# A two-layer hybrid decoder step: the order of work around the ConvFFN's openings, pairs, stage change and round changes

## The chip, the cores and the metric

The kernel runs on one core of a Trainium2 chip. The metric is the device time of one execution in microseconds (us), median of several runs. TensorE (PE) multiplies, VectorE (DVE), ScalarE (ACT) and GpSimd (POOL) do elementwise work, and SyncE (SP) issues nearly all DMA transfers.

## The reference, cut to what matters

Two layers run for a prompt of 1024 tokens and 64 sample tokens together. Each layer is a mixer (attention and a recurrence in layer 0, a chunk MLP in layer 1) followed by a gated ConvFFN, which is what the change touches:

```python
def conv_ffn(xn, buf, w_g, w_u, w_c, b_c, w_d):
    g = xn @ w_g                                  # 1024 -> 3072
    gc, new_buf = causal_dwconv(g, buf, w_c, b_c) # 3 taps along the tokens
    return (jax.nn.gelu(gc) * (xn @ w_u)) @ w_d, new_buf
...
yp = yp + conv_ffn(rmsnorm(yp, g_ffn[l]), ...)
```

All is float32. The outputs are the two activations and the caches and states.

## The kernel before, in words

Activations lie with features on partitions: eight tiles of 128 features by 1088 tokens. A float32 product is made of three products of rounded operands: every operand is split into a high part (a ScalarE copy to fp32r, "hi") and a low part (the rest, a subtraction, "lo"), and hi·hi, lo·hi and hi·lo are added in PSUM.

The ConvFFN uses a seven-product scheme (Winograd's form of Strassen's) over 2 × 2 blocks. A **job** is one such scheme: seven **groups** of matmuls i = 0..6, in `multiply` (line 2190), with the activation operands B21, B11, T1, T2, B22, NT4, T3 and seven weight blocks. Four weight blocks come from the sums S1 to S4 of the raw weight quarters (`block_sum`, L2115). `block_hi` (L2288, ScalarE) and `block_lo` (L2121) split them; VectorE takes the lows 2, 3, 4, 6 and GpSimd 0, 1, 5. Jobs 0 to 23 are the up and gate stage: 12 pairs, an even job for the gate and an odd one for up, 24 matmuls a group. Jobs 24 to 39 are the down stage: four rounds of four jobs, 18 matmuls a group. Sums go to PSUM banks 6 and 7, except those of job 0, which GpSimd makes into two SBUF buffers (`first_sums`, L2084 to L2093).

**Opening.** While the projection ahead (`Output`, matmuls of L148) ends, VectorE evacuates its tiles (L1827), and makes the sums T1, T3, T2, NT4 of the activation halves (L2440, L2428, L2434, L2458); L2449 makes their lows. The reciprocal root of the mean square comes from squares (L1652 on ScalarE, added by GpSimd at L1661) and three matmuls with ones (L1669) into banks 6 and 7.

**Pair.** Results of a group leave PSUM by a ScalarE copy (L2307) and a VectorE addition (`add_out`, L2480). The gate is scaled (L2486), goes through the convolution (first tap on ScalarE, L2325; the other two in `conv_taps`, L2492 and L2494; samples, L2505 to L2509), gelu (L2336), a scaling on GpSimd (L2127), and is multiplied with the up half in `hidden_tile` (L2514). GpSimd makes the four sums of the hidden halves (`hidden_sum`, L2524), and SP stores tiles and sums in DRAM.

**Down stage.** For each round seven pieces (3 × 544 columns) are loaded back (L2026), split by `piece_hi` (L2345, ScalarE) and `piece_lo` (L2132; VectorE makes five, GpSimd T2 and NT4), and VectorE adds each group's result to the residual tile (`add_residual`, L2543), whose tiles are reloaded from `x_spill` (L1994). Job 27, 31, 35 end a round; the next round's pieces are split during them.

The order on each engine is written out by hand, and each engine runs its list strictly in order; semaphores tie the lists together. SP's list is `sync`. A group of PE waits for its weight lows, for its operand lows, and for the VectorE addition that frees the PSUM bank which it writes:

```python
if i in (1, 4, 6):
    dve.wait_ge(self.dve_out, base + {1: 1, 4: 4, 6: 6}[i])   # add_residual
...
elif i == 3:
    pe.wait_ge(self.dve_out, dve + 1)                         # up/gate stage: after add_out(n, 1)
elif i in (0, 1):
    pe.wait_ge(self.dve_out, dve - 1 + i)                     # down stage
```

## Time and profile before

| what | value |
|---|---|
| median of 3 runs | 2687.48 us (2686.31 to 2687.71) |
| profiled execution, its own time | 2689.28 us |
| its span | 2687.6 us, mean granted TensorE clock 0.974 |
| busy: PE, DVE, ACT, POOL | 2494.0, 1790.8, 1149.8, 1038.4 us |
| FFN of layer 0: opening, pairs, down stage | from about 628, from about 700, 1189 to 1494 us |
| FFN of layer 1: the same | from about 1805, from about 1877, 2365 to 2679 us |

Times in rows count from the start of the span. A value in brackets is how long the engine had been idle before the instruction and what ended that idle time. The granted clock is 1.00 at 2.4 GHz and 0.50 at 1.2 GHz.

### The profile page before, as it was taken

The numbers are of one execution on the slowest core, as the hardware profiler recorded it, in microseconds if no ns is written. First come the engines' busy times: TensorE is split into PE (matmuls) and PEld (weight loads), VectorE is DVE, ScalarE is ACT, GpSimd is POOL, SyncE is SP. The second block draws the span as 40 slices with busy tenths as digits, with TensorE's granted clock in tenths as the row PEclk, the third lists the DMA queues.
The fourth block names the chain that finished last, engine by engine and source line by source line (L and its number), as shares of the span: only waits on it lengthen the run. The fifth ranks groups of instructions, "written<-read, shape, count | busy, mean of one in ns | idle before, by whom it ended". The sixth has DMA issues, their size and how long they took to land.

```text
span 2687.6 us, 46186 instructions
## 1 busy us (share of the span) xinstructions
PE 2494.0 (93%) x18693; PEld 2387.7 (89%) x18693; DVE 1790.8 (67%) x2118; ACT 1149.8 (43%) x1851; POOL 1038.4 (39%) x663
## 2 busy tenths in 40 slices
PE   8999998897899999988988999996999999988888
PEld 7878876697899999988988999996999999988888
DVE  6456566547687777786667434548677768777774
ACT  5575666434444444443223433434443444433331
POOL 3244332225344545452223412244535455442221
PEclk9999999998999999999999999998999999998999
DMA  5101118642223222255332211121223232274322
GB/s 177 56 24 43 42 32 283 232 151 81 73 79 109 90 94 101 82 189 185 121 112 78 57 35 52 55 90 56 94 89 106 77 106 93 99 258 136 127 81 79
DMA packets 214176, 276.98 MB, mean 103 GB/s; under 512 B 11437, under 2 KB 158998, under 8 KB 210894
## 3 DMA queue, kind: packets, MB, share of 16 engines
q1 hardware_dynamic: 212910, 271.83, 30.4%
q8 instruction: 149, 2.44, 0.4%
q10 hardware_dynamic: 576, 2.10, 0.2%
q14 instruction: 61, 0.50, 0.1%
q0 software_dynamic: 480, 0.11, 0.0%
HBM read 203.57 MB, written 70.43 MB: 102 GB/s over the span
## 4 chain that ended last, share of the span: by engine, by line
PE 60%; DVE 10%; issue 5%; DMA 2%; ACT 1%; POOL 1%; SPq 0%; ACTq 0%; DVEq 0%; POOLq 0%
PE psum_all L2190 46%; PE psum_all L2798 6%; PE psum_all L148 6%; DVE x_residual L2492 2%; DVE psum_all L2115 1%; DVE x_residual L2486 1%; DVE x_residual L2480 1%; DMA pair_raw_ffn<-in_w_down_dram 1%; POOL down_x_ffn L2132 1%; DVE down_x_ffn L2132 1%; DVE ffn_x_sums L2440 0%; DVE x_residual L2543 0%; PE psum_all L2850 0%; PE psum_all L2814 0%; DVE block_s L2121 0%
## 5 line engine op out<-in xcount | busy, mean ns | idle before, releaser
L2190 PE MATMUL psum_all<-ffn_x,blocks 128*128 128x272 f32 x5760 | 748.6, 291 | 65.3 <-DVE x_residual L2480 34.6
L2190 PEld LDWEIGHTS psum_all<-ffn_x,blocks 128*128 128x128 f32 x5760 | 738.2, 191 | 70.9 <-issue 55.3
L2190 PE MATMUL psum_all<-down_x_ffn,blocks_down 128*128 128x272 f32 x2880 | 395.6, 299 | 74.4 <-issue 44.4
L2190 PEld LDWEIGHTS psum_all<-down_x_ffn,blocks_down 128*128 128x128 f32 x2880 | 386.4, 199 | 80.3 <-issue 79.9
L2307 ACT COPY x_residual<-psum_all 128x544 f32<-128x544 f32 x192 | 117.8, 614 | 403.5 <-PE psum_all L2190 399.1
L2543 DVE TENSOR_TENSOR x_residual<-x_residual,psum_all 128x544 f32<-128x544 f32 (+1 forms) x224 | 178.6, 798 | 152.9 <-PE psum_all L2190 151.5
L113 POOL TENSOR_TENSOR w_lo_part<-w_raw,w_hi_part 128x1024 fp32r<-128x1024 f32 x52 | 126.9, 2440 | 356.0 <-ACT w_hi_part L97 356.0
L2480 DVE TENSOR_TENSOR x_residual<-x_residual,psum_all 128x544 f32<-128x544 f32 x144 | 130.4, 906 | 123.6 <-PE psum_all L2190 119.8
L2127 POOL TENSOR_TENSOR x_residual<-x_residual,rms_scale 128x1088 f32<-128x1088 f32 x48 | 134.8, 2809 | 180.6 <-ACT x_residual L2336 180.6
L2121 DVE TENSOR_TENSOR blocks<-psum_all,blocks 128x512 fp32r<-128x512 f32 x138 | 94.9, 688 | 118.4 <-ACT blocks L2288 118.4
L2798 PE MATMUL psum_all<-operand_a,w_hi_part 128*128 128x364 f32 (+1 forms) x672 | 169.9, 330 | 0.0
L909 PE MATMUL psum_all<-in_hi_even,w_hi_part 128*128 128x384 f32 (+1 forms) x456 | 157.0, 344 | 1.2 <-DVE xb_padded L1430 0.6
L1363 POOL TENSOR_TENSOR take_then_weights<-take_then_weights,x_residual 128x511 f32<-128x511 f32 (+3 forms) x96 | 95.0, 1001 | 159.3 <-DVE x_residual L1395 119.1
L2190 PE MATMUL psum_all<-ffn_x,block_a 128*128 128x272 f32 x1152 | 152.4, 288 | 0.0
L2190 PE MATMUL psum_all<-ffn_x,block_s 128*128 128x272 f32 x1152 | 151.9, 287 | 0.0
L909 PE MATMUL psum_all<-in_lo_even,w_hi_part 128*128 128x384 f32 (+1 forms) x456 | 149.3, 327 | 0.0
L909 PE MATMUL psum_all<-in_hi_even,w_lo_part 128*128 128x384 f32 (+1 forms) x456 | 149.0, 327 | 0.0
L2524 POOL TENSOR_TENSOR x_residual<-x_residual 128x544 f32<-128x544 f32 x96 | 144.3, 1503 | 9.8 <-DVE x_residual L2514 2.6
L2190 PEld LDWEIGHTS psum_all<-ffn_x,block_a 128*128 128x128 f32 x1152 | 147.2, 188 | 0.5
L2190 PEld LDWEIGHTS psum_all<-ffn_x,block_s 128*128 128x128 f32 x1152 | 147.0, 188 | 0.0
L1395 DVE TENSOR_TENSOR_SCAN x_residual<-x_residual,all_ones 128x512 f32<-128x512 f32 (+3 forms) x96 | 91.8, 990 | 73.2 <-ACT x_residual L1183 73.2
L2798 PEld LDWEIGHTS psum_all<-operand_a,w_hi_part 128*128 128x128 f32 x672 | 119.3, 188 | 0.5
(372 smaller groups left out, 4835.5 us busy)
## 6 DMA issues: line engine op xcount, KB each, us to landing
staging_ffn<-hidden_spill SPq DMA_DIRECT2D x54, 816.0 KB, 6.1
hidden_spill<-x_residual SPq DMA_DIRECT2D x24, 1088.0 KB, 4.0
w_raw<-in_w_gate_dram SPq DMA_DIRECT2D x24, 1024.0 KB, 5.6
x_residual<-in_w_up_dram SPq DMA_DIRECT2D x24, 1024.0 KB, 5.2
pages<-in_cache_k_dram SPq DMA_DIRECT2D x64, 256.0 KB, 3.6
pages<-in_cache_v_dram SPq DMA_DIRECT2D x64, 256.0 KB, 5.6
x_spill<-x_residual SPq DMA_DIRECT2D x24, 546.0 KB, 5.5
x_residual<-x_spill SPq DMA_DIRECT2D x24, 546.0 KB, 5.8
```

The lines of the kernel that those rows point to most:

```text
L113: pool.tensor_tensor(dst if dst is not None else self.lo[:, par, :], self.raw[:, par, :], (hi if hi is not None else self.hi[:, par, :]).b ...
L148: mm = pe.matmul(bank[:, c, 0:width(c)], w, x[:, chunk(c)], start=(k == 0 and step == 0), stop=(k == last and step == 2))
L909: mm = pe.matmul(bank(key, 0, b - a), wt[:, n % 2, col], xt[:, k, a:b], start=k == 0 and s == 0, stop=k == KT - 1 and s == 2)
L1363: pool.tensor_tensor(t[:, 0:n - 1], t[:, 0:n - 1], k[:, 1:n], ALU.mult).then_inc(weighted, 1)
L2121: eng.tensor_tensor(self.block(n, i, 1).rearrange("p (q c) -> p q c", c=P), self.source(n, i), self.block(n, i, 0).bitcast(F32).rearrange( ...
L2127: pool.tensor_tensor(self.conv[:, r, :], self.conv[:, r, :], self.core.rb[:, 0:USED], ALU.mult).then_inc(self.gr_ready, 1)
L2190: mm = pe.matmul(self.core.ps[:, b + h, 0:HB], wt[:, q * P:(q + 1) * P], xt[:, q, HB * h:HB * (h + 1)], start=first and at == 0, stop=at = ...
L2307: act.copy(self.half(self.target(n, r), h).rearrange("p (h n) -> p h n", h=2), self.group(name)).then_inc(self.act_out, 1)
L2480: dve.tensor_tensor(dst, dst, src, ALU.add).then_inc(self.dve_out, 1)
L2524: pool.tensor_tensor(dst, x, y, op).then_inc(self.hsum, 1)
L2543: dve.tensor_tensor(dst, dst, src, ALU.add).then_inc(self.dve_out, 1)
L2798: mm = pe.matmul(self.core.ps[:, self.lane_bank(f), 0:width(c)], wm[:, is_u, col], xm[:, k, chunk(c)], start=k == 0 and s == 0, stop=k == ...
```

## The change

It reorders the hand-written lists and moves some instructions to another engine; all results are the same.

- Job 0's sums are made by VectorE into banks 6 and 7 (`first_weights_dve`, ahead of the evacuation of tile 6), with its lows 2, 3, 4, 6 on VectorE too. GpSimd keeps lows 0, 1, 5. The sums of squares go to the banks of group "d". The square scratch moves by 1024 bytes, so that it no longer overlaps block 3.
- Job 1's sums and most of its lows move into the opening's list. The load of job 1 waits for the first NT4 sum, which is now that of tile 1, instead of all four.
- `conv_taps` becomes `conv_tap`, one tap each: the addition of the up job's group 1 stands between the two taps of the first half, and sums and lows between those of the second.
- The last pair's hidden tiles and hidden sums go to the end of VectorE's list for job 24 (`down_first`).
- All piece lows are VectorE's. At a round change B21, B11, T1, T2 are made during the last job of the round, B22, NT4, T3 during the first of the next, whose sums for the job after come later.
- SP loads pieces 7 to 10 (the next round's first four) before the last pair's stores.

```diff
@@ Output.vector
         for m in range(KT):
-            if m == KT - 1:
+            if m == KT - 2:
+                self.ffn.first_weights_dve(dve)
+            elif m == KT - 1:
                 self.ffn.open_dve(dve)
@@ Ffn.sync
-        sp.wait_ge(self.sum_lead, self.T_MADE[NT4][3])
+        sp.wait_ge(self.sum_lead, self.T_MADE[NT4][0])
         self.load(sp, 1)
...
         self.load_next(sp, n + 2)
+        for g in range(7, 11):
+            self.load_piece(sp, g)
         self.store_hidden(sp, PAIRS - 1)
...
-            if r < ROUNDS - 1:
+            if 0 < r < ROUNDS - 1:
                 for i in range(4):
                     self.load_piece(sp, 7 * (r + 1) + i)
@@ Ffn.gpsimd
+        self.block_lo(pool, 0, 0)
+        self.block_lo(pool, 0, 1)
         self.add_squares(pool, KT - 2)
-        pool.wait_ge(*self.out.job_done(KT - 2))
-        self.first_sums(pool, "S1")
-        for i in (1, 0, 2):
-            self.block_lo(pool, 0, i)
         pool.wait_ge(self.act_lead, self.T_HI[T1])
...
-        self.first_sums(pool, "S4")
         self.add_squares(pool, KT - 1)
-        pool.wait_ge(self.s_sum, KT - 1)
-        for i in (3, 4, 5):
-            self.block_lo(pool, 0, i)
+        self.block_lo(pool, 0, 5)
...
-        self.block_lo(pool, 0, 6)
...
-                if n == JOBS1 - 1 and i in (5, 6):
-                    self.piece_lo(pool, 0, (T2, NT4)[i - 5])
-                elif turn and i in (T2, NT4):
-                    self.piece_lo(pool, r + 1, i)
@@ Ffn.opening (PE)
         self.multiply(pe, 0, 3)
+        pe.wait_ge(self.act_out, 1)
         self.sums_pe(pe, (0, 1))
...
         pe.wait_ge(self.t2_lo, 2)
+        pe.wait_ge(self.s_root, 3)
         self.multiply(pe, 0, 5)
@@ Ffn.opening_act
+        for i in range(4):
+            self.block_hi(act, 0, i)
         self.tile_act(act, KT - 2)
-        self.block_hi(act, 0, 1)
-        self.block_hi(act, 0, 0)
...
-        self.block_hi(act, 0, 2)
-        self.tile_act(act, KT - 1)
-        self.block_hi(act, 0, 3)
         act.wait_ge(self.sum_lead, self.T_MADE[T2][2])
         act.activation(self.operand(0, T2, 0)[:, 0:3], self.temp(T2)[:, 0:3], ACT.Copy).then_inc(self.act_lead, 1)
+        self.tile_act(act, KT - 1)
@@ Ffn.first_weights_dve, new
+        self.block_sum(dve, 0, "S1")
+        self.block_sum(dve, 0, "S2")
+        self.block_lo(dve, 0, 2)
+        self.block_sum(dve, 0, "S4")
+        self.block_lo(dve, 0, 3)
+        self.block_sum(dve, 0, "S3")
@@ Ffn.opening_dve
+        dve.wait_ge(self.sum_lead, self.T_MADE[NT4][3])
         self.part_lo(dve, T2, 0, self.t2_lo)
+        self.block_lo(dve, 0, 4)
         self.tile_lo(dve, KT - 1, 1, B22, 1)
-        dve.wait_ge(self.sum_lead, self.T_MADE[NT4][3])
         self.part_lo(dve, NT4, 0, self.t2_lo)
+        self.block_lo(dve, 0, 6)
+        self.block_sum(dve, 1, "S1")
+        self.block_sum(dve, 1, "S2")
         self.add_out(dve, 0, 4)
         self.part_lo(dve, T3, 2, self.t3_lo)
+        self.block_lo(dve, 1, 2)
+        self.block_sum(dve, 1, "S4")
+        self.block_lo(dve, 1, 3)
+        self.block_sum(dve, 1, "S3")
         self.add_out(dve, 0, 6)
@@ Ffn.vector, a pair
-            self.conv_taps(dve, o, t, 0)
+            self.conv_tap(dve, o, t, 0, 1)
             self.add_out(dve, u, 1)
+            self.conv_tap(dve, o, t, 0, 0)
             self.conv_samples(dve, o, t, 0)
             self.block_lo(dve, u + 1, 2)
             self.block_sum(dve, u + 1, "S4")
-            self.conv_taps(dve, o, t, 1)
+            self.conv_tap(dve, o, t, 1, 1)
             self.block_lo(dve, u + 1, 3)
             self.block_sum(dve, u + 1, "S3")
+            self.conv_tap(dve, o, t, 1, 0)
...
-            self.hidden_tile(dve, t, 0)
+            else:
+                self.hidden_tile(dve, t, 0)
@@ Ffn.vector, jobs 25 to 39
+            turn, turned = p == QUARTERS - 1 and r < ROUNDS - 1, p == 0
+            if not turned:
+                self.next_sums(dve, n + 1)
             for i in range(7):
                 self.add_residual(dve, n, i)
...
+                if turn and i == 1:
+                    self.piece_lo(dve, r + 1, B21)
+                elif turn and i == 2:
+                    self.piece_lo(dve, r + 1, B11)
+                elif turned and i == 1:
+                    self.piece_lo(dve, r, B22)
+                elif turned and i == 2:
+                    self.piece_lo(dve, r, NT4)
+                    self.next_sums(dve, n + 1)
+                elif turned and i == 3:
+                    self.piece_lo(dve, r, T3)
+                self.next_lo(dve, n + 1, i - (1 if turned else 0))
+                if turn and i == 4:
+                    self.piece_lo(dve, r + 1, T1)
+                elif turn and i == 6:
+                    self.piece_lo(dve, r + 1, T2)
+                if turned and i == 6:
+                    self.next_lo(dve, n + 1, 6)
@@ Ffn.down_first, new: job 24 (n = JOBS1), t = PAIRS - 1
+        self.piece_lo(dve, 0, T1)
+        self.add_residual(dve, n, 0)
+        self.add_residual(dve, n, 1)
+        self.piece_lo(dve, 0, T2)
+        self.piece_lo(dve, 0, B22)
+        self.add_residual(dve, n, 2)
+        self.piece_lo(dve, 0, NT4)
+        self.add_residual(dve, n, 3)
+        self.piece_lo(dve, 0, T3)
+        self.next_sums(dve, n + 1)
+        self.next_lo(dve, n + 1, 2)
...
+        self.hidden_tile(dve, t, 0)
+        self.hidden_tile(dve, t, 1)
+        for i in (T1, T3, T2, NT4):
+            self.hidden_sum(dve, t, i)
```

## Rows read from the trace of the kernel before

**Rows 1.** The page, costliest groups: busy, mean ns of one | idle before, releaser.

```profile
L2190 PE MATMUL psum_all<-ffn_x,blocks 128*128 128x272 f32 x5760 | 748.6, 291 | 65.3 <-DVE x_residual L2480 34.6
L2190 PE MATMUL psum_all<-down_x_ffn,blocks_down 128*128 128x272 f32 x2880 | 395.6, 299 | 74.4 <-issue 44.4
```

**Rows 2.** Waits of PE, 706 to 1180 us: total, times, longest.

```profile
PE psum_all L2190 <- DVE x_residual L2480: 9.3, 9, 1.0
```

**Rows 3.** Timeline of PE, opening and job 1: start, duration, what, idle before.

```profile
650.80 7.93 PE L2190 MATMUL psum_all<-ffn_x,blocks 128*128 128x272 f32 x48 [7.24 <-DVE x_residual L1827]
666.01 5.73 PE L2190 MATMUL psum_all<-ffn_x,blocks 128*128 128x272 f32 x24 [7.28 <-DVE ffn_x L2449]
...
682.42 9.16 PE L2190 MATMUL psum_all<-ffn_x,blocks 128*128 128x272 f32 x72
700.11 1.24 PE L2190 MATMUL psum_all<-ffn_x,blocks 128*128 128x272 f32 x4 [8.54 <-DVE x_residual L2480]
```

**Rows 4.** Windows: us, busy PE, PEld, DVE, ACT, POOL, granted clock, DMA.

```profile
662.00:671.00 9.00, 4.99 (x22) 5.02 (x23) 9.00 (x4) 5.64 (x6) 6.82 (x4) 0.50 0.69 216
872.00:915.00 43.00, 41.97 (x336) 41.78 (x335) 32.84 (x37) 17.74 (x34) 21.00 (x12) 1.00 0.27 95
```

**Rows 5.** Timeline of PE, stage change of layer 0.

```profile
1199.93 6.35 PE L2190 MATMUL psum_all<-down_x_ffn,blocks_down 128*128 128x272 f32 x36 [4.08 <-DVE down_x_ffn L2132]
...
1246.29 7.23 PE L2190 MATMUL psum_all<-down_x_ffn,blocks_down 128*128 128x272 f32 x36 [6.96 <-DVE x_residual L2543]
```

**Rows 6.** Timeline of PE, first round change.

```profile
1281.71 8.55 PE L2190 MATMUL psum_all<-down_x_ffn,blocks_down 128*128 128x272 f32 x51 [7.10 <-issue]
```

**Rows 7.** Timeline of VectorE, opening.

```profile
632.33 6.71 DVE L2440 SCALAR_TENSOR_TENSOR ffn_x_sums<-x_residual,params,ffn_x_sums 128x544 f32<-128x544 f32 x4 [1.90 <-ACT ffn_x_sums L2354]
...
649.46 1.28 DVE L1827 TENSOR_TENSOR x_residual<-x_residual,psum_all 128x1092 f32<-128x1092 f32 x1
...
658.17 2.86 DVE L2458 SCALAR_TENSOR_TENSOR ffn_x_sums<-x_residual,params,ffn_x_sums 128x544 f32<-128x544 f32 x4
...
662.50 3.42 DVE L2449 TENSOR_TENSOR ffn_x<-ffn_x_sums,ffn_x 128x2176 fp32r<-128x2176 f32 x1
```

**Rows 8.** Timeline of GpSimd, opening.

```profile
633.20 1.77 POOL L2084 TENSOR_TENSOR block_sums_a<-w_raw 128x512 f32<-128x512 f32 x1
...
662.36 1.27 POOL L2121 TENSOR_TENSOR blocks<-block_sums_b,blocks 128x512 fp32r<-128x512 f32 x1 [4.70 <-ACT blocks L2288]
```

**Rows 9.** DMA issued at 619.16 us: KB, us to landing.

```profile
w_raw<-in_w_gate_dram SPq DMA_DIRECT2D x1, 1024.0 KB, 6.7
```

**Rows 10.** Timeline of VectorE, job 1.

```profile
683.83 0.69 DVE L2115 TENSOR_TENSOR psum_all<-x_residual 128x512 f32<-128x512 f32 x1
...
688.90 0.70 DVE L2115 TENSOR_TENSOR psum_all<-x_residual 128x512 f32<-128x512 f32 x1
...
696.61 1.34 DVE L2492 SCALAR_TENSOR_TENSOR x_residual<-x_residual,ffn_params 128x1088 f32<-128x1088 f32 x1
...
699.25 0.71 DVE L2480 TENSOR_TENSOR x_residual<-x_residual,psum_all 128x544 f32<-128x544 f32 x1
```

**Rows 11.** Timeline of VectorE, a later pair.

```profile
870.05 2.38 DVE L2492 SCALAR_TENSOR_TENSOR x_residual<-x_residual,ffn_params 128x1088 f32<-128x1088 f32 x1
872.46 2.46 DVE L2494 SCALAR_TENSOR_TENSOR x_residual<-x_residual,ffn_params 128x1088 f32<-128x1088 f32 x1
874.85 0.71 DVE L2480 TENSOR_TENSOR x_residual<-x_residual,psum_all 128x544 f32<-128x544 f32 x1
```

**Rows 12.** The chain that ended last, at the stage change: start, us, what.

```profile
1230.33 13.18 DMA pair_raw_ffn<-in_w_down_dram
```

**Rows 13.** Timeline of VectorE, first round change.

```profile
1275.85 5.14 DVE L2132 TENSOR_TENSOR down_x_ffn<-staging_ffn,down_x_ffn 128x1632 fp32r<-128x1632 f32 x1
...
1283.39 1.85 DVE L2132 TENSOR_TENSOR down_x_ffn<-staging_ffn,down_x_ffn 128x1632 fp32r<-128x1632 f32 x1
```

**Rows 14.** Timeline of GpSimd, first round change.

```profile
1275.64 3.62 POOL L2132 TENSOR_TENSOR down_x_ffn<-staging_ffn,down_x_ffn 128x1632 fp32r<-128x1632 f32 x1
```

More of the change, by code:

```diff
@@ L1895, in x_lo_done @@
     def x_lo_done(self, r, i):
-        if i in (T2, NT4):
-            return self.x_lo_pool, 2 * r + (T2, NT4).index(i) + 1
-        return self.x_lo, 5 * r + (B21, B11, T1, B22, T3).index(i) + 1
+        return self.x_lo, 7 * r + i + 1
     def gain(self, m):
@@ L2374, in opening_act @@
         self.copy_out(act, 0, 2)
-        act.wait_ge(*self.out.job_done(KT - 1))
-        self.block_hi(act, 0, 5)
         act.wait_ge(self.sum_lead, self.T_MADE[T3][3])
         act.activation(self.operand(0, T3, 0), self.temp(T3), ACT.Copy).then_inc(self.act_lead, 1)
-        self.block_hi(act, 0, 6)
         self.copy_out(act, 0, 3)
         self.roots_act(act)
-        self.block_hi(act, 1, 0)
-        self.block_hi(act, 1, 1)
+        for i in range(4):
+            self.block_hi(act, 1, i)
         self.copy_out(act, 0, 5)
-        for i in range(2, 7):
+        for i in range(4, 7):
             self.block_hi(act, 1, i)
@@ L2455, in opening_dve @@
         self.t2_sum(dve, 3)
-        for q in range(4):
+        for at, q in enumerate((1, 0, 2, 3)):
             dve.wait_ge(self.sum_lead, self.T_MADE[T2][q])
@@ L2618, in vector @@
-                if p == QUARTERS - 1 and r < ROUNDS - 1 and i not in (T2, NT4):
-                    self.piece_lo(dve, r + 1, i)
+                if turn and i == 1:
[9 more added lines that the diff above has]
+                    self.piece_lo(dve, r, T3)
```

165 lines of the change are left out of this document (66 added, 99 removed).

## The prediction

> **What bounds the kernel now.** I read the page's list of costliest groups first. The block products of both ConvFFN layers is one helper, line 2190, and TensorE (PE) sat idle before its matmuls for 65.3 us on the up and gate side and 74.4 us on the down side [rows 1]. The busy shares alone (PE 93%) hide this: PE is the engine that sets the end, and what this change can give is in its holes. The waits of PE in the stretch of the steady pairs show one kind of hole, nine waits of 1.0 us for the VectorE addition of line 2480 [rows 2]. The timeline of PE then places the large ones, once in each layer: 7.24 us and 7.28 us in the opening and 8.54 us in job 1 [rows 3]; 4.08 us, some small ones and 6.96 us at the stage change [rows 5]; 7.10 us at each of three round changes [rows 6]. The other layer has the same holes (its stage change has 4.7 in place of 4.1).
>
> Each large hole costs twice. After it a group of 24 matmuls that takes 3.0 us in a row of groups (72 in 9.16) takes 5.73 us [rows 3], and the granted clock of that stretch is 0.50, so 1.2 GHz in place of 2.4 [rows 4]; the first 51 matmuls after a round change take 8.55 us [rows 6], where 36 at full clock take 4.7. I count 2.0 to 2.7 us of slow clock behind each hole of over 6 us.
>
> **Opening.** Three parts act together. (a) The first job's sums go to VectorE, ahead of the evacuation of tile 6. The load of its weights is issued at 619.16 and takes 6.7 us [rows 9], so the six VectorE steps start at 625.9. The same chain for job 1 (S1 to S3 with ScalarE's copies between) takes from 683.83 to 689.60, 5.8 us [rows 10]. It ends at 631.7, while job 6 of the projection was finished by 627.5: tile 6 is evacuated 4.1 us later. From there the same scale, square and temporary copies follow, and the first T1 sum starts at about 635.3 against 632.33 [rows 7]. That is 3.0 us lost, and all that is queued behind is ten sums and the evacuation of tile 7.
>
> (b) Those ten sums are VectorE instructions with two SBUF inputs. Beside a busy GpSimd four take 6.71 us, 1.68 each; with GpSimd idle four take 2.86, 0.72 each [rows 7]. GpSimd's own 512-wide step takes 1.77 beside them and 1.27 alone [rows 8]: each waits for the other, and an instruction of VectorE that reads one side from PSUM is not slowed (0.69 us [rows 10]). After the change GpSimd has only one squares addition and one part low in this stretch, about 2.5 us each. Ten sums are 7.2 us and two blocks 3.5 us, so tile 7 is evacuated at 635.3 + 10.8 = 646.1 instead of 649.46 [rows 7]: 3.4 us gained. PE's idle before job 0's second group falls from 7.24 to about 4.7.
>
> (c) From that evacuation to the end of T2's low (662.50 + 3.42 = 665.92) was 16.5 us. The squares still block once; the GpSimd low of block 5 now meets the last NT4 sum, but no longer the 2176-wide low (3.42 beside a 1.27 us GpSimd step; about 2.4 alone). I get 15.6 us, so group 3 of job 0 starts at 661.7 against 666.01. PE is then idle for about 8 us, and I keep the slow clock there. Group 5 now waits for the three logarithms, because the sums of squares use its bank: 0.9 us, ends of a range 0 and 1.5. Job 1 starts at 679.2 against 682.42 [rows 3].
>
> In job 1 group 3 waits for the addition of line 2480 at 699.25 [rows 10]. Before it VectorE did the six sums and lows of job 1 (5.8 us), which now run in job 0, started by an up load that goes out three sums earlier, and the second tap, which moves behind it (1.34). With job 0's end at 679.2 plus 0.1 my list of VectorE's work is: addition 1.3, scaling 1.3 plus 0.2 of a GpSimd low, two lows 1.3, two sums 1.4, scaling 1.3, first tap 1.3, addition 0.7, together 8.7: ready at 688.0. Group 2 ends at 688.2. The 8.54 us hole and its 2.6 us of slow clock go. Group 4 begins at 691.3 instead of 705.7: **14.4 us a layer, 28.8 in all** (20 to 34).
>
> **Pairs.** The addition that PE waits for starts at 874.85, right behind two taps of 2.38 and 2.46 us; these take about 1.35 when no GpSimd low meets them [rows 10, 11]. Group 2 was finished at 874.7. With one tap moved behind it, the addition ends at 873.1, so the wait ends 1.6 us before it is needed. The pace falls from 43.27 us per pair to between 42.0 (14 groups of 3.0) and 42.16, what pairs without the hole took. Next in line is the second tap, which can meet the first gate scaling of GpSimd (2.55 us); it delays the gelu of the second half, and with it the hidden tile that stands ahead of the next pair's first addition. That had 1.4 us of slack. VectorE is busy 32.84 of 43 us [rows 4], so it can keep the pace. Seventeen pairs in the two layers show the hole: 17 × 1.2 = **20 us** (0 to 21.6).
>
> **Stage change.** The 6.96 us hole is a late load: issued at 1230.33, it needs 13.18 us behind eight other transfers [rows 12], and VectorE's residual additions stand behind the sum that waits for it. SP issued it only after the stores of the last pair, four reloads and four pieces. The four pieces now go out before the stores, at about 1201 to 1208, when their places are free. The stores come later than before: hidden tiles and four sums (4 × 0.72) are now at VectorE's end of job 24. Walking VectorE's new list from the last pair (seven piece lows of 1.85 [rows 13], seven additions, six block steps, two hidden tiles, four sums), with up to 1 us for each GpSimd low met, I get T1's group at 1198.3 (was 1199.93 [rows 5]), job 25 at 1214.6 (1215.80), its group 3 at 1225.6 (1223.23), so 2.4 us lost by then; the store lands at 1226 and the load at about 1237, before group 3 of job 26 at 1241.4 (was 1246.29, at half clock). With the slow clock gone, 7.4 us are gained. The other layer's hole of 4.7 shrinks too: 10.5. **Together 18 us** (6 to 24).
>
> **Round changes.** At 1275.64 GpSimd starts a piece low of 3.62 us, which takes VectorE 1.85 [rows 13, 14]. VectorE's own low from 1275.85 is blocked and takes 5.14, and behind it in the queue is the residual addition that frees the bank of job 28's first group: PE starts at 1281.71 after 7.10 us of idle [rows 6]. Eight groups there (job 27, first of 28) take 28.1 us against 8 × 2.26 = 18.1: 10.0 us over, of which 2 is clock. After the change all seven lows are on VectorE, spread over two jobs, and B22, NT4 and T3 come after the turn. VectorE's work over the two jobs is 12 additions at 0.64, two at 1.21, eight block lows at 0.48, eight sums at 0.6 and seven piece lows at 1.77, which is 31.1 us beside 31.6 us of PE. So it is nearly full, and each GpSimd block low (six of them, about 1.0 us by the 1.27 for 512 columns [rows 8]) that meets a long low shows; bounds are none met, 0 us over, and all six met, 6 us. My walk gives 0.6 us before job 28, 0.8 us before T3's group and 1.1 us before job 29: 2.5 over. Gain 7.4 each, six of them: **44 us** (24 to 59).
>
> The Trainium skill speaks against this part (SBUF — State Buffer, Who interferes with whom): a VectorE instruction with two SBUF inputs and a GpSimd one that reads SBUF exclude each other whole, and the one issued second waits. With GpSimd first each time, that is the 6 us end, not 2.5; the blocked 5.14 us low [rows 13] agrees with the rule.
>
> **Sum.** 28.8 + 20 + 18 + 44 = 111. The profiled execution took 2689.28 us (span 2687.6), 1.8 above the median of 2687.48; so 2578 from it and 2576 to 2577 in runs like the shown ones. I take 2578.
>
> **Rivals.**
> 1. VectorE is full at the round changes. For it: 31.1 of 31.6 us. Every GpSimd low is met, the excess is 6 us instead of 2.5: 2578 + 6 × 3.5 = 2599.
> 2. The pair hole only moves: the first addition of the next pair becomes late behind the hidden tile. For it: 1.4 us of slack against a gate scaling of 2.55. Against: that tile is bound by GpSimd's second scaling, whose start depends on a gelu that hardly moves. 2578 + 20 = 2598.
> 3. The clock. Holes of about 4 us remain in the opening and at the stage change, and would slow four more groups that matter by 2 us: 2587. The 4.08 us hole is followed by 36 matmuls in 6.35 us [rows 5], so it can happen; mostly VectorE is then the later one anyway. The Trainium skill (TensorE: Matmul & The Clock Gate, Why this matters for your kernels) warns of pauses between bursts of matmuls, after which the clock is lowered; this rival is what it would do here.
> 4. Better than said: meetings rarely happen and turns cost under 1 us: 2560 or less. The floor is all 139.7 us of idle [rows 1] and about 25 of clock, some 2524.
> 5. Slower than before: the gate scaling (2.55) and the second tap meet, gelu and hidden tile slip, and every pair waits for its first addition. It costs 22 × (slip − 1.4), as eleven pairs a layer follow another. It has to take back 111 − 20 = 91 us, so it decides from a slip of 5.5 us on; one meeting is 2.55. At 6 us it gives 2699.
> 6. The change does not act: the sums in the opening start later by the 4.1 us and everything queued behind holds PE as before, pairs are bound by gelu: within 0.2% of before.
>
> **How the numbers follow.** The forecast 0.55 (own range 2564 to 2592); rival 1 0.17; rival 2 0.10; rival 3 0.06; rival 4 0.08; rival 5 0.03; rival 6 0.01. The range goes from 2554 to 2614: it takes in rivals 1 to 3 and part of 4, and rivals 1 and 2 together at 2619 only just lie outside. Faster by over 0.2% (5 us, about what a measurement can tell) has 0.96, within 0.01, slower 0.03.
>
> **What the profile after would show.** Opening: the T1 sums at 0.72 each except where a squares addition stands beside them; tile 7 evacuated near 646; job 1's group 3 with under 1 us of idle. Pairs: no wait of PE for line 2480's successor, 42.0 to 42.2 us a pair. Stage change: the load for job 27 landing in under 11 us and before its addition is needed; VectorE's four hidden sums just ahead of job 25's additions. Rounds: PE idle in pieces of about 1 us, full clock throughout, GpSimd without lows of 1632 elements. I am wrong if PE's idle in the two layers stays above 60 us, or if the lows on VectorE take over 2.5 us on average.

## The result and the profile after

The changed kernel takes **2579.11 us** (median of 4 runs, 2573.71 to 2584.72) against 2686.89 us of the kernel before on the same chip: ratio 0.9604, 95% interval 0.9576 to 0.9631. Run once more, on the chip of v_opening, v_rounds and v_stage below, it gave 2581.26 us, ratio 0.9609 (0.9596 to 0.9622). Each experiment below has its ratio to the kernel before on its own chip; compared with these two ratios, it tells what the edit costs or gives. The forecast was 2578, faster with 0.96. The profiled execution took 2576.1 us (span 2574.4), 113.2 less than the 2689.28 of the one before.

The page, costliest groups, same columns as [rows 1]; the helper is now line 2153:

```profile
L2153 PE MATMUL psum_all<-ffn_x,blocks 128*128 128x272 f32 x5760 | 737.6, 289 | 22.6 <-DVE ffn_x L2416 13.8
L2153 PE MATMUL psum_all<-down_x_ffn,blocks_down 128*128 128x272 f32 x2880 | 376.9, 292 | 24.4 <-DVE x_residual L2519 11.5
```

Idle before these block products fell from 139.7 to 47.0 us (140.5 to 51.5 with the groups of block_a and block_s, which stand in rows of their own), and the time in them by 29.7 us. The mean granted clock rose from 0.974 to 0.991, so I take these 29.7 us for slow clock that went with the holes. Timeline of PE in the opening of layer 0 (start, duration, idle before and its releaser), against [rows 3]:

```profile
637.60 3.18 PE L2153 MATMUL psum_all<-ffn_x,blocks 128*128 128x272 f32 x24
643.47 6.40 PE L2153 MATMUL psum_all<-ffn_x,blocks 128*128 128x272 f32 x48 [2.69 <-DVE x_residual L1828]
658.09 5.47 PE L2153 MATMUL psum_all<-ffn_x,blocks 128*128 128x272 f32 x24 [8.23 <-DVE ffn_x L2416]
...
669.04 3.24 PE L2153 MATMUL psum_all<-ffn_x,block_a 128*128 128x272 f32 x24 [0.65 <-ACT rms_scale L1676]
672.12 3.16 PE L2153 MATMUL psum_all<-ffn_x,block_s 128*128 128x272 f32 x24
675.12 15.16 PE L2153 MATMUL psum_all<-ffn_x,blocks 128*128 128x272 f32 x120
```

The first hole is 2.69 us instead of 7.24. The one before group 3 is 8.23 instead of 7.28 and ends 8 us earlier. In layer 1 the two are 4.91 and 5.61. Job 1 runs its first five groups in one row of 120 matmuls: its 8.54 us hole is gone. The same for the pairs (waits: total, times, longest), the stage change and the first round change, against [rows 2, 5, 6]:

```profile
PE psum_all L2153 <- DVE down_x_ffn L2106: 4.0, 1, 4.0
PE psum_all L2153 <- ACT x_residual L2268: 1.0, 1, 1.0
PE psum_all L2153 <- DVE x_residual L2455: 0.4, 1, 0.4
```

```profile
1169.26 9.60 PE L2153 MATMUL psum_all<-down_x_ffn,blocks_down 128*128 128x272 f32 x54 [4.00 <-DVE down_x_ffn L2106]
...
1185.38 8.49 PE L2153 MATMUL psum_all<-down_x_ffn,blocks_down 128*128 128x272 f32 x54 [2.02 <-DVE x_residual L2519]
1195.88 0.85 PE L2233 MATMUL psum_all<-identity,new_state_columns 128*72 128x128 f32 x6 [2.02 <-DVE x_residual L2519]
...
1205.89 11.43 PE L2153 MATMUL psum_all<-down_x_ffn,blocks_down 128*128 128x272 f32 x90
...
1238.04 11.51 PE L2153 MATMUL psum_all<-down_x_ffn,blocks_down 128*128 128x272 f32 x90 [0.45 <-issue]
...
1252.35 2.50 PE L2153 MATMUL psum_all<-down_x_ffn,block_s 128*128 128x272 f32 x18 [0.54 <-DVE down_x_ffn L2106]
1255.83 6.41 PE L2153 MATMUL psum_all<-down_x_ffn,blocks_down 128*128 128x272 f32 x49 [0.98 <-DVE x_residual L2519]
```

Between 700 and 1180 us nine waits of 1.0 us for the VectorE addition became one of 0.4 (the waits of 4.0 and 1.0 us stand in job 24, behind the pairs). The late load's hole in job 26 (6.96) is gone. A **turn** is a round change: each has three pieces of idle, 2.0 us together, where 7.10 and slow clock were.

Cut at the starts of groups, the two profiled executions differ so (us, layer 0 / layer 1; the first line from the end of the projection, the last to the end of job 39):

| stretch | before | after | gain, both | forecast |
|---|---|---|---|---|
| opening, to job 1's group 4 | 66.2 / 66.3 | 49.4 / 51.6 | 31.5 | 28.8 |
| pairs, to job 24 | 483.8 / 482.1 | 472.8 / 473.5 | 19.5 | 20 |
| stage change, job 24 to 27 | 68.4 / 69.8 | 61.7 / 61.7 | 14.8 | 18 |
| jobs 27 to 39 | 236.4 / 241.9 | 213.9 / 218.6 | 45.7 | 44 |

That is 111.5; the other 1.7 lie ahead of the first projection's end (639.5 against 637.8), in work that the change doesn't touch.

### The profile page after: what moved, and what is told of

It reads as the page before. It is cut to its first block, busy times and chain, and to the rows that moved or that the text cites. A ratio compares the mean times of both kernels' runs of the same rounds, so it can differ in the third digit from the quotient of the medians.

```text
span 2574.4 us, 46180 instructions
## 1 busy us (share of the span) xinstructions
PE 2466.7 (96%) x18693; PEld 2364.2 (92%) x18693; DVE 1765.6 (69%) x2158; ACT 1148.4 (45%) x1851; POOL 961.9 (37%) x623
## 4 chain that ended last, share of the span: by engine, by line
PE 64%; DVE 9%; issue 3%; ACT 1%; POOL 1%; DMA 1%; SPq 0%; DVEq 0%; ACTq 0%; POOLq 0%
PE psum_all L2153 52%; PE psum_all L2810 7%; PE psum_all L148 3%; DVE down_x_ffn L2106 2%; DVE psum_all L2091 1%; DVE x_residual L2519 1%; DVE x_residual L2470 1%; DMA w_raw<-in_w_gate_dram 1%; PE psum_all L2862 0%; PE psum_all L2826 0%; POOL rms_scale L1661 0%; DVE blocks_down L2095 0%; POOL w_lo_part L113 0%; DVE ffn_x_sums L2407 0%; PE psum_all L2850 0%
## 5 line engine op out<-in xcount | busy, mean ns | idle before, releaser
L2153 PE MATMUL psum_all<-ffn_x,blocks 128*128 128x272 f32 x5760 | 737.6, 289 | 22.6 <-DVE ffn_x L2416 13.8
L2153 PE MATMUL psum_all<-down_x_ffn,blocks_down 128*128 128x272 f32 x2880 | 376.9, 292 | 24.4 <-DVE x_residual L2519 11.5
L2153 PEld LDWEIGHTS psum_all<-down_x_ffn,blocks_down 128*128 128x128 f32 x2880 | 370.3, 191 | 28.7 <-issue 27.9
L2470 DVE SCALAR_TENSOR_TENSOR x_residual<-x_residual,ffn_params 128x1088 f32<-128x1088 f32 x96 | 215.2, 2242 | 0.0
L2101 POOL TENSOR_TENSOR x_residual<-x_residual,rms_scale 128x1088 f32<-128x1088 f32 x48 | 153.2, 3191 | 151.7 <-ACT x_residual L2297 151.7
L2500 POOL TENSOR_TENSOR x_residual<-x_residual 128x544 f32<-128x544 f32 x88 | 130.1, 1479 | 6.3
```

The costliest lines, as they stand in the source:

```text
L2101: pool.tensor_tensor(self.conv[:, r, :], self.conv[:, r, :], self.core.rb[:, 0:USED], ALU.mult).then_inc(self.gr_ready, 1)
L2153: mm = pe.matmul(self.core.ps[:, b + h, 0:HB], wt[:, q * P:(q + 1) * P], xt[:, q, HB * h:HB * (h + 1)], start=first and at == 0, stop=at = ...
L2470: o.did(dve.scalar_tensor_tensor(gc, gb[:, j:j + USED], par[:, f + FT * j:f + FT * j + 1], gc, ALU.mult, ALU.add))
L2500: eng.tensor_tensor(dst, x, y, op).then_inc(self.hsum, 1)
```

## The experiments

All are edits of the changed kernel. "Step" is the time from one group's start to another's in the profiled execution; a turn's step is job 27's first group to job 29's second, 36.5 us in the changed kernel at all six turns, 44.0 before at the first.

**One part undone: the tap (u_taps).**

```
             self.conv_tap(dve, o, t, 0, 1)
-            self.add_out(dve, u, 1)
             self.conv_tap(dve, o, t, 0, 0)
+            self.add_out(dve, u, 1)
```

> One part undone: both taps of the first row stand ahead of the addition of group 1 again (everything else as in the changed kernel). Theory (the tap in front of the addition is the whole of the pair gain): the second tap costs 1.34 us to 2.5 us of VectorE before that addition, PE waits about 1.0 us for it at group 3 in most pairs, the pace goes from 42.0 back towards 43.3 us in some 17 pairs of both layers, and the time rises by 17 to 22 us. Rival (something else of the new order gave the pairs their pace, the tap is covered): pace stays at 42.0 and the time rises by less than 5 us.

2608.38 us, ratio 0.9706 (0.9688 to 0.9724): 26 to 27 us more, which is above the 17 to 22 expected. Waits of PE in the pairs of layer 0, VectorE before one of them, and PE in job 1:

```profile
PE psum_all L2153 <- DVE x_residual L2455: 8.2, 8, 1.0
```

```profile
728.78 4.88 DVE L2470 SCALAR_TENSOR_TENSOR x_residual<-x_residual,ffn_params 128x1088 f32<-128x1088 f32 x2
733.58 0.71 DVE L2455 TENSOR_TENSOR x_residual<-x_residual,psum_all 128x544 f32<-128x544 f32 x1
```

```profile
689.67 4.61 PE L2153 MATMUL psum_all<-ffn_x,blocks 128*128 128x272 f32 x23 [2.04 <-DVE x_residual L2455]
```

The waits are back and the pair stretches are 20.9 us longer, as the first theory has it. A further 7.6 us are in job 1, whose step to group 4 goes from 12.0 to 15.8 in both layers: there the same edit brings back a hole of 2.0 us with slow clock behind it, which the expectation had left out. Before the change this step was 23.3, so the tap is 3.8 of the 11.3 us that it lost. (The two profiled executions differ by more than the medians: the one shown of the changed kernel is 3 us below its median, with one opening in the short form that "again" tells of.)

**The round changes taken apart (u_pool_lows, u_old_order).** The first gives T2's and NT4's lows back to GpSimd, the second keeps all seven on VectorE and puts them where the others stood before:

```
+                elif turn and i in (T2, NT4):       # gpsimd()
+                    self.piece_lo(pool, r + 1, i)
```

```
+            self.next_sums(dve, n + 1)              # vector(), the whole job
+            for i in range(7):
+                self.add_residual(dve, n, i)
+                self.next_lo(dve, n + 1, i)
+                if turn:
+                    self.piece_lo(dve, r + 1, i)
```

> One part undone: the lows of the pieces T2 and NT4 are made on GpSimd again, at the places in its list where they stood; VectorE keeps the new, spread order of the other five. Theory (what cost the time is the engine: a GpSimd low of 3.6 us holds up VectorE's SBUF work): the lows that meet it take 4 to 5 us on VectorE, a hole of 2 to 6 us with slow clock comes back at each of six turns and another at each stage change, and the time rises by 18 to 45 us. Rival (what gained is the spreading over two jobs, which takes the lows from in front of the additions that free banks; which engine makes them hardly counts): within 6 us of the changed kernel, or faster, since VectorE loses 3.7 us of work per turn.

> One part undone: at the three turns of each layer VectorE makes all seven piece lows, but each right behind the addition of its own group in the last job of the old round, and the next sums stand first in the job after (the list of the kernel before with T2 and NT4 added). The stage change keeps the new list. Theory (place counts as well as engine): seven lows of 1.85 us and the usual 9.4 us of one job are 22 us against 15.8 us of PE, and NT4's piece, which lands some 5 us into the new job, stands ahead of the addition that frees the bank of job 28's first group: holes of 5 to 8 us with 2 us of slow clock, six times, the time rises by 25 to 60 us. Rival (only GpSimd's lock mattered): VectorE's slack in the neighbouring jobs takes the lows, the time rises by less than 8 us.

2593.91 us (0.9654, 0.9632 to 0.9676) and 2596.29 us (0.9664, 0.9648 to 0.9680). VectorE, GpSimd and PE of the first at the turn:

```profile
1239.40 4.62 DVE L2110 TENSOR_TENSOR down_x_ffn<-staging_ffn,down_x_ffn 128x1632 fp32r<-128x1632 f32 x1
1243.94 2.10 DVE L2528 TENSOR_TENSOR x_residual<-x_residual,psum_all 128x544 f32<-128x544 f32 x2
```

```profile
1238.59 3.71 POOL L2110 TENSOR_TENSOR down_x_ffn<-staging_ffn,down_x_ffn 128x1632 fp32r<-128x1632 f32 x1 [4.92 <-ACT down_x_ffn L2315]
```

```profile
1244.75 12.81 PE L2162 MATMUL psum_all<-down_x_ffn,blocks_down 128*128 128x272 f32 x90 [3.23 <-issue]
```

A low of VectorE (1.85 us alone) waits for GpSimd's and takes 4.62, and the addition behind it frees the bank late. In the second kernel no low is held up, but the additions stand behind lows that nobody waits for yet:

```profile
1246.80 2.50 PE L2153 MATMUL psum_all<-down_x_ffn,blocks_down 128*128 128x272 f32 x18 [2.70 <-issue]
```

Jobs 27 to 39 of both layers take 12.0 us more with GpSimd's lows and 17.1 more with the old places; with both, which is the kernel before, 45.7. So both causes are real, and their costs don't simply add: with the lows at GpSimd in a spread list, or all on VectorE in the old list, a turn has one hole of 2.7 to 3.2 us and at most two small ones; together they give 7.1 and more slow clock. Whole, the two kernels are 12 to 13 and 15 to 16 us slower than the changed one. Both costs are below the ranges that I had expected of them (18 to 45 and 25 to 60), and above what either rival allows.

**The early pieces (u_pieces).**

```
-        for g in range(7, 11):
-            self.load_piece(sp, g)
...
-            if 0 < r < ROUNDS - 1:
+            if r < ROUNDS - 1:
```

> One part undone: pieces 7 to 10 are loaded behind the last pair's stores and the four reloads again. Theory (the early issue is what removed the hole of 6.96 us at the stage change): the load of job 27 goes out some 2 us later and behind four more transfers, lands at 13 us from its issue instead of 7.9, VectorE's additions of job 26 stand behind its first sum, and PE has a hole of 3 to 6 us before group 3 of job 26 with slow clock behind it; the time rises by 8 to 18 us for the two layers. Rival (the late hidden sums and the order of job 24 gave the gain, the transfer is now covered anyway): less than 3 us.

2596.26 us (0.9665, 0.9647 to 0.9683). The load of job 27:

```profile
pair_raw_ffn<-in_w_down_dram SPq DMA_DIRECT2D x1, 768.0 KB, 13.2
```

The same load in the changed kernel:

```profile
pair_raw_ffn<-in_w_down_dram SPq DMA_DIRECT2D x1, 768.0 KB, 7.9
```

VectorE and PE of this kernel:

```profile
1220.46 0.57 DVE L2089 TENSOR_TENSOR psum_all<-pair_raw_ffn 128x384 f32<-128x384 f32 x1 [9.14 <-DMA pair_raw_ffn<-in_w_down_dram]
```

```profile
1223.22 3.06 PE L2151 MATMUL psum_all<-down_x_ffn,blocks_down 128*128 128x272 f32 x12 [6.93 <-DVE x_residual L2517]
```

The old hole is back to 0.1 us. Counted from job 24's start, the load is issued 3.1 us later and takes 5.3 us longer. The stage change takes 72.6 and 70.9 us, 20 us more than 61.7 twice, and also more than the 68.4 and 69.8 of the kernel before. The medians say 15 to 17 us. The early issue of four transfers is thus all of this part's gain (14.8); without it the rest of the new stage change gains nothing. The 5 us that it costs in these two profiles are not shown to be more than run-to-run spread: by the medians it is 0 to 2.

**The last pair's sums (u_hidden).** Tiles at their old places, the four sums on GpSimd:

```
-                if up and i == 6 and n < JOBS1 - 1:
+                if up and i == 6:                   # gpsimd(), T1's sum
...
-        for i in (T1, T3, T2, NT4):                 # down_first()
-            self.hidden_sum(dve, t, i)
```

> One part undone: the last pair's hidden tiles stand at their old places on VectorE and its four sums are on GpSimd again; the early pieces and everything else stay. Theory (GpSimd's sums hold the lock beside seven piece lows of 1.85 us, and VectorE's two tiles take 2.6 us where it is fullest): job 24 becomes 2 to 6 us longer, the idle of 2.0 to 3.7 us before the state rows' turning goes, and the store goes out earlier; from job 24's start to job 27's the time changes by minus 1 to plus 5 us a layer. Rival (putting the sums late gained nothing, since the four sums on VectorE themselves hold the addition that PE waits for): 2 us or more faster a layer.

2577.43 us (0.9603, 0.9586 to 0.9620). PE:

```profile
1188.15 9.63 PE L2153 MATMUL psum_all<-down_x_ffn,blocks_down 128*128 128x272 f32 x54 [4.79 <-DVE x_residual L2519]
1197.62 0.82 PE L2233 MATMUL psum_all<-identity,new_state_columns 128*72 128x128 f32 x6
```

The hole before job 25 grows from 2.02 to 4.79 us and the one before the state rows goes. Job 24 to 27 takes 62.0 and 62.2 us (61.7 twice; 64.2 and 61.1 in the later run of the changed kernel), within the minus 1 to plus 5 a layer of the theory. Putting these sums late moves idle time and gains nothing that can be measured.

**A cost put back (u_busy).** Four 512-column subtractions on GpSimd in the opening, their result unused:

```
+        for k in range(4):
+            if k:
+                pool.wait_ge(self.dummy, k)
+            pool.tensor_tensor(self.mem.dummy..., self.part(0, 0, 0), self.part(0, 0, 1), ALU.subtract)...
```

> One suspected cost put back: GpSimd makes four 512-column subtractions of its own (into an unused tile, the result is not used) between the two squares additions in the opening, where before it made job 0's sums. Theory (VectorE's sums with two SBUF inputs take 1.68 us in place of 0.77 while GpSimd works in SBUF, each waiting for the other): four to eight of the ten sums take 1.6 us or more, tile 7 is evacuated 3 to 6 us later, and the time rises by 4 to 10 us for the two layers. Rival (VectorE keeps the lock, as it did for six sums in a row beside GpSimd's part low that took 4.42 us, and GpSimd's work is what gets longer): the sums stay near 0.77 us, and the time rises by less than 3 us.

2588.28 us (0.9640, 0.9625 to 0.9656): 8 to 10 us more. VectorE and GpSimd; the changed kernel has 4.62 us for the first row and 2.16 for the second:

```profile
634.37 7.75 DVE L2413 SCALAR_TENSOR_TENSOR ffn_x_sums<-x_residual,params,ffn_x_sums 128x544 f32<-128x544 f32 x4 [0.85 <-ACT ffn_x_sums L2321]
642.04 5.40 DVE L2393 SCALAR_TENSOR_TENSOR ffn_x_sums<-x_residual,params,ffn_x_sums 128x544 f32<-128x544 f32 x3
```

```profile
636.27 6.97 POOL L2118 TENSOR_TENSOR dummy_sum<-w_raw 128x512 f32<-128x512 f32 x4
```

The step from job 0's first group to its second becomes 12.2 and 12.3 us, from 5.9 and 8.1 (10.5 in both layers of the kernel before). The sums alternate with GpSimd's steps again, 1.8 to 1.9 us each: keeping these four steps out of this stretch is worth 4 to 6 us a layer.

**The kernel as it is, once more (again).**

> The changed kernel itself once more, unaltered, on the chip of the next three. It gives their base and shows how often the opening and the stage change fall into the longer of the two forms seen so far: the step from job 0's first group to its second at 5.9 or 8.1 us, and the idle before the turning of the state rows at 2.0 or 3.7 us. Theory (two races for VectorE's and GpSimd's lock explain the spread of 2573.7 to 2584.7 us): both forms appear again and the runs spread by 5 to 11 us. Rival (the spread lies ahead of the two layers' feed-forward parts): those steps repeat to 0.1 us and the spread stands in the part before them.

2581.26 us (2577.84 to 2582.89). The spread is the 5 us of the theory. Over the nine profiled executions whose opening is the changed kernel's, the first step is 5.76 to 6.01 us in seven of 18 openings and 8.04 to 8.22 in eleven, never between. The idle before the state rows is 3.71 us in layer 0 of this run and 1.96 in layer 1. Both forms of the first step stand in the first profile. GpSimd and VectorE, layer 0:

```profile
640.17 4.42 POOL L2115 TENSOR_TENSOR ffn_x<-ffn_x_sums,ffn_x 128x1088 fp32r<-128x1088 f32 x1 [4.82 <-ACT ffn_x L2322]
```

```profile
640.04 2.16 DVE L2393 SCALAR_TENSOR_TENSOR ffn_x_sums<-x_residual,params,ffn_x_sums 128x544 f32<-128x544 f32 x3
642.14 1.27 DVE L1828 TENSOR_TENSOR x_residual<-x_residual,psum_all 128x1092 f32<-128x1092 f32 x1
```

and layer 1:

```profile
1760.80 2.98 POOL L2115 TENSOR_TENSOR ffn_x<-ffn_x_sums,ffn_x 128x1088 fp32r<-128x1088 f32 x1 [4.82 <-ACT ffn_x L2322]
```

```profile
1760.66 4.39 DVE L2393 SCALAR_TENSOR_TENSOR ffn_x_sums<-x_residual,params,ffn_x_sums 128x544 f32<-128x544 f32 x3
```

In layer 0 three sums and the evacuation of tile 7 go first and GpSimd's part low takes 4.42; in layer 1 that low gets in between the sums and tile 7 is 2.2 us later.

**The opening in another order (v_opening).** VectorE makes all of T1's low behind that evacuation, and GpSimd adds the squares after T2's low:

```
+            if m == KT - 1:
+                self.ffn.part_lo(dve, T1, 0, self.ffn.t1_lo)
...
+        pool.wait_ge(self.t2_lo, 1)
         self.add_squares(pool, KT - 1)
...
         self.part_lo(dve, T2, 0, self.t2_lo)
+        self.add_out(dve, 0, 1)
```

> New order for the opening alone: VectorE makes all of T1's low right behind the evacuation of tile 7 (GpSimd no part of it), GpSimd adds the last squares and makes block 5's low only after T2's low, the T2 low stands ahead of the first addition, and ScalarE copies group 0 out ahead of block 4 to 6's his. Theory (the 14.6 us from the second group of job 0 to group 3 are the lock's turns: 2.5 us for GpSimd's part low, 2.6 for the squares, 1.0 for block 5): this step falls to 10 to 12 us, and the step before it is always 5.9 us and never 8.1; 6 to 11 us in all. Rival (ScalarE's his and copies are the later ones, or the squares become late for the logarithms of group 5): what is gained before group 3 is lost before group 4 or 5, within 2 us of the changed kernel.

**2566.50 us** (2565.57 to 2567.82; 0.9557, 0.9544 to 0.9570), 14 to 15 us faster than the changed kernel on the same chip, where 6 to 11 were expected. PE:

```profile
644.25 2.52 PE L2153 MATMUL psum_all<-ffn_x,blocks 128*128 128x272 f32 x18 [2.65 <-DVE x_residual L1828]
647.28 4.04 PE L2153 MATMUL psum_all<-ffn_x,blocks 128*128 128x272 f32 x30 [0.52 <-DVE ffn_x L2382]
654.83 5.77 PE L2153 MATMUL psum_all<-ffn_x,blocks 128*128 128x272 f32 x24 [3.52 <-DVE x_residual L2454]
```

The first step is 5.7 to 5.9 in this run and in the two below that share the edit (six openings), the second 10.6 in place of 14.6. The runs spread over 2.3 us here and 4.5 and 3.8 in those two, against 5.1 and 11.0 in the two measurements of the changed kernel. The race can account for up to 2.3 us in each of two openings. That it makes most of the spread is not shown: u_old_order and v_stage keep the race and spread over only 3.0 and 3.9 us. What makes the rest I have not traced.

**The turns and the stage change in another order (v_rounds, v_stage).** In v_rounds T1's low stands behind the addition of group 5, T3's ahead of the next sums, and group 5's addition of the turned job ahead of a low and a sum. In v_stage T1's low stands ahead of block 6's low of job 24, and additions ahead of the sums in jobs 24 to 26.

> Turned kernel order for the round changes alone: T1's low behind the last addition but one of the old round, T3's low ahead of the next sums, and the addition that frees job 29's first bank ahead of two lows and a sum. Theory (the 2.0 us of idle per turn is order within VectorE's queue, which has 31.1 us of work for 31.6 us): the pieces of 0.45, 0.54 and 0.98 us go, 2.0 us in each of six turns, 8 to 12 us in all. Rival (VectorE is simply full there, so the idle moves to job 29): less than 3 us.

> New order for the stage change alone: T1's piece low ahead of block 6's low of job 24, the hi of that block ahead of ScalarE's wait for piece B22, the addition of group 5 of job 24 ahead of two block steps, the last hidden sum behind the first addition of job 25, and the sums of jobs 26 and 27 behind the first two additions of the jobs before. Theory (the four remaining holes of 2.0 to 4.0 us and the slow clock behind them are queue order on VectorE and ScalarE): 5 to 9 us a layer, 10 to 16 us in all. Rival (the pieces' transfers, which land at intervals of about 4.5 us, or VectorE's sum of work set the pace of job 24): below 4 us in all.

2575.57 us (0.9591, 0.9578 to 0.9604) and 2574.31 us (0.9585, 0.9572 to 0.9598): 5 to 6 and 6 to 7 us faster than the changed kernel. v_rounds at the turn:

```profile
1261.20 2.49 PE L2153 MATMUL psum_all<-down_x_ffn,blocks_down 128*128 128x272 f32 x18 [1.15 <-DVE x_residual L2519]
1264.04 4.13 PE L2153 MATMUL psum_all<-down_x_ffn,blocks_down 128*128 128x272 f32 x31 [0.35 <-DVE x_residual L2519]
```

Two of the three pieces went and 1.5 us moved to job 29, so this lies between theory and rival. Jobs 27 to 39 are 5.4 us shorter. In v_stage the 4.00 us hole of T1's group becomes 1.43 and 1.19, and those of 2 us stay; it too lies between its theory (10 to 16) and its rival (below 4).

**All together, and the idle followed once more (v_all, v_best).** In v_all the turned job's last three additions stand ahead of most of the block steps for the next job. v_best also puts the sums behind the first two additions in the job after each turn, job 25's first addition ahead of the hidden tiles and its second between them, and the sums that wait for job 27's load behind four additions of job 26:

```
-                    self.next_sums(dve, n + 1)        # turned, i == 3
+                elif turned and i == 4:
+                    self.next_sums(dve, n + 1)
+                elif turned and i == 5:
+                    self.next_lo(dve, n + 1, 2)
+                elif turned and i == 6:
+                    for k in (3, 4, 6):
+                        self.next_lo(dve, n + 1, k)
...
+                elif p == 1 and n > JOBS1 + 1 and i == 1:   # v_best alone
+                    self.next_sums(dve, n + 1)
```

> The new opening of the run before, and a further order for both the stage change and the turns: there the six additions of the turned job stand ahead of the two or three block lows and sums that stood between them, so nothing that PE waits for is behind a step that only the next job needs; the lows of the next job's blocks come last. At the stage change the two first additions of job 25 also stand ahead of the hidden sums. Theory (the idle that v_rounds left, 1.15 and 0.35 us a turn, is queue order and not VectorE's total work): turns fall from 36.5 to about 34.2 us for the sixteen groups counted from job 27 to 29, 14 us in all; the stage change gives 8 to 14, the opening the 15 it gave alone: 2537 to 2550 us. Rival (VectorE's total of 31.1 us is the limit, with what GpSimd's lows take): turns stay at 35.6 and the gains of the three do not add up: 2555 us or more.

> The kernel of the run before with its three remaining places put right: the sums of the job after next stand behind the first two additions in the jobs after each turn, where the idle of 0.9 to 1.4 us had moved; the two first additions of job 25 stand ahead of and between the hidden tiles instead of behind them; and the sums that wait for job 27's transfer stand behind four additions of job 26. Theory (all three are additions queued behind steps that nothing waits for yet; VectorE has 6 us to spare in jobs 29 and 30): four jobs from 27 to 31 take 63.3 us, the bound of 28 groups, in place of 64.3 (6 us in all), and the idle of 2.76 and 0.7 to 1.3 us around the state rows falls below 1 us in each layer (5 us, with the clock): 2541 to 2549 us. Rival (VectorE is full and the idle only moves on again, to job 30 or to job 26's additions): 2553 to 2558 us.

2556.09 us (0.9518, 0.9504 to 0.9531) and **2546.58 us** (2544.41 to 2548.16; 0.9486, 0.9473 to 0.9499), 33 to 35 us faster than the changed kernel. PE of v_all behind the turn, then the window of v_best over four jobs with a turn in them (columns as in [rows 4]):

```profile
1254.24 4.00 PE L2153 MATMUL psum_all<-down_x_ffn,blocks_down 128*128 128x272 f32 x30 [1.03 <-DVE x_residual L2518]
```

```profile
1212.00:1275.00 63.00, 63.00 (x506) 63.00 (x505) 52.54 (x69) 23.60 (x35) 16.36 (x12) 1.00 0.44 144
```

v_all missed its 2537 to 2550 us. Its turns did better than expected, 33.8 us at all six, but a hole of 1.03 us appeared behind each: jobs 27 to 39 are 10.0 us shorter where 14 were expected, and the stage change 4.9 where 8 to 14 were. In v_best, which kept within its range, the turn's step is 33.8 us again and PE has no idle in the window. VectorE is busy 52.5 of 63 us there. At the stage change the five microseconds expected of v_best did not come: its two holes went and one of 3.70 us before group 4 of job 25 took their place (58.0 and 61.2 us, against 58.6 and 60.0 in v_all).

## Why the prediction was right, and where it was off

**Opening** (28.8, measured 31.5). From job 1's start to its group 4 both layers took 12.0 us, where the forecast had 12.1: the 8.54 us hole is gone. The two-input sums take 0.77 us, group 3's hole is kept with its slow clock, and the logarithms cost 0.65 us where I had 0.9. u_busy shows that an empty GpSimd queue keeps the sums short. u_taps shows that the tap gives 3.8 of the 11.3 us a layer in job 1; that the rest comes from the six sums and lows which moved into job 0 is argued, and no run undoes that part by itself. One number was a mean of a thing that has no mean: tile 7 "near 646", 6.6 us behind the projection, is one of the race's two forms; the first layer had the other, 4.4. What lies above the forecast is luck: with the long form in both layers, in the second run of the same kernel, the part gave 29.6.

**Pairs** (20, measured 19.5). The named hole, the named cure, no other wait taking its place, and nine of eleven steps from pair to pair in each layer at 42.0 us. VectorE's second tap does meet GpSimd's scaling (rival 2), 3.69 us in the last pair, and no pair waits for it.

**Stage change** (18, measured 14.8). For layer 0 I had the groups to 0.7 us: counted from job 24's start T1's group at 8.9 (measured 9.3), job 25 at 25.2 (25.5), its group 3 at 36.2 (measured 36.9), job 27 at 61.0 (61.7). The load landed 7.9 us after its issue, not 11, and it needed this: the addition that group 3 of job 26 waits for ended 0.4 us before it. The term that was mis-sized is the other layer, 10.5 forecast and 8.1 found: I had not walked its list. B11's low meets GpSimd's scaling there, 4.21 us in place of 1.85, and PE waits 2.80; before job 25 it waits 3.60, where layer 0 has 2.02:

```profile
2283.29 4.21 DVE L2106 TENSOR_TENSOR down_x_ffn<-staging_ffn,down_x_ffn 128x1632 fp32r<-128x1632 f32 x1
```

```profile
2281.62 4.16 POOL L2101 TENSOR_TENSOR x_residual<-x_residual,rms_scale 128x1088 f32<-128x1088 f32 x1
```

```profile
2288.80 4.77 PE L2153 MATMUL psum_all<-down_x_ffn,blocks_down 128*128 128x272 f32 x36 [2.80 <-DVE x_residual L2455]
2307.66 8.54 PE L2153 MATMUL psum_all<-down_x_ffn,blocks_down 128*128 128x272 f32 x54 [3.60 <-DVE x_residual L2519]
```

What I had not seen is how the part is made up: the transfers alone are worth as much as the whole part, and the late hidden sums nothing that can be measured.

**Round changes** (44, measured 45.7). The step of a turn, 15 groups, is 36.5 us against a bound of 33.8 (15 at the pace of a row without idle), 2.7 over where the forecast had 2.5; 2.0 of these are idle, in the three places named. But VectorE's 31.1 us of work for 31.6 is refuted as a limit: v_best does the same work in another order, part of it later, and PE has no idle at the turns. The sum was taken over two jobs, and the two jobs after have room. What was left was order.

**The total.** The four parts are off by +2.7, -0.5, -3.2 and +1.7 us. That the sum, 111.5, lies 0.5 us from the forecast is cancellation, and so luck; the parts themselves are each within 3.2 us. Neither sign of being wrong came: PE's idle in the two layers is 51.5 us (under 60), and the 56 piece lows on VectorE take 1.95 us on average (under 2.5).

**The rivals.** VectorE full at the turns: refuted by v_best. The pair hole moving: no. The clock at holes of about 4 us: it fell behind the 4.00 at 1169 us and even behind the 2.02 at 1185 (54 matmuls in 8.49 us where 6.9 would do); this is inside the measured 14.8. How much of what is missing to 18 it explains I have not separated. Slower: nothing of it.

## What to carry to other kernels

Where one engine both frees the accumulators of the current job and prepares the next one, put every freeing step ahead of every preparing step that has slack, and follow the idle to the next job before calling the engine full: here, between the changed kernel and v_best, order alone took another 16.6 us out of jobs 27 to 39. A transfer that is needed late is still worth issuing before a burst of others. Undo the parts of a bundled change one at a time: one of these gave nothing (the late hidden sums), one carried the whole gain of its stage (the early pieces), and two at the turns gave more together than one by one.

## What the runs showed of the hardware

GpSimd does not always get its turn at SBUF by asking first. In layer 0 its part low starts at 640.17, ahead of the second and third of VectorE's sums in the row at 640.04, and took 4.42 us while the three sums took 2.16 together; in layer 1 the same low got in between them and the three took 4.39. The Trainium skill (SBUF — State Buffer, Who interferes with whom) says that the order of issue decides. By the starts in the profile layer 1 agrees with that and layer 0 does not, and the measurement stands. VectorE's instructions follow each other without a pause in both. In both layers GpSimd's low starts 0.13 to 0.14 us behind VectorE's first sum. Why it falls one way or the other is open.

The length of an idle time does not by itself tell the granted clock behind it. In the changed kernel's profile two idle times of 2.02 us lie 10 us apart. Behind the first, at 1185.38, 54 matmuls took 8.49 us where 6.9 would do, and the mean granted clock from 1184 to 1200 us was 0.89. Behind the second, before the state rows, it was 1.00:

```profile
1184.00:1200.00 16.00, 12.54 (x85) 12.12 (x86) 14.50 (x21) 3.58 (x8) 3.62 (x3) 0.89 0.51 188
1196.00:1205.00 9.00, 8.94 (x71) 8.70 (x71) 5.98 (x10) 2.36 (x5) 0.51 (x1) 1.00 0.81 295
```

A longer one can pass too: behind the 2.70 us of u_old_order's turn 18 matmuls took 2.50 us, the full pace. In the second run of the changed kernel the idle before the state rows was 3.71 us, and a granted clock of 0.51 followed, that is 1.2 GHz in place of 2.4:

```profile
1198.00:1205.00 7.00, 5.44 (x25) 5.29 (x26) 3.86 (x7) 1.34 (x3) 0.00 (x0) 0.51 0.68 246
```

From job 25's first group to job 26's group 5 it was 31.8 us the first time and 34.2 the second. What decides the clock at idle times of 2 to 4 us these runs leave open.
